# Second block of a two-block transformer on one core: a new order of its 48 attention steps and of the slabs beside them

## What is computed

```python
def hybrid_mixer(u, cos, sin, ...):
    (dq, dk, dv, nq, kc_, vc_, ks_, vs_, kw_, vw_, ngate, mgate) = jnp.split(u @ w_in, split_at, axis=-1)
    dq, dk = apply_rope(dq, c4, s4), apply_rope(dk, c4, s4)
    y_a = differential_attention(dq, dk, dv, lam)          # p[0] - lam * p[1], causal, 4 heads of 2
    y_a = rms_norm(y_a, diff_subln_g) * (1.0 - lam_init) @ w_branch_a
    nq = apply_rope(nq, c3, s3)
    k_cmp = compress(apply_rope(kc_), cmp_pe_k, cmp_k_w1, cmp_k_w2)   # silu(blk @ w1) @ w2, 31 blocks of 32 tokens
    v_cmp = compress(vc_, cmp_pe_v, cmp_v_w1, cmp_v_w2)
    o_c, o_s, o_w = nsa_attention(nq, k_cmp, v_cmp, k_sel, vs_, k_win, vw_)
    y_b = g[:, :, 0] * o_c + g[:, :, 1] * o_s + g[:, :, 2] * o_w
    return (mg[:, :, 0] * y_a + mg[:, :, 1] * (y_b @ w_branch_b)) @ w_out
```

## Time and profile before

| | us |
|---|---|
| median of 3 runs | 2106.61 (2105.53 to 2108.7) |
| the profiled execution | 2107.49 |
| its span in the trace | 2105.7 |
| TensorE busy with matmuls | 2037.0 (97% of the span) |
| VectorE / ScalarE / GpSimd busy | 967.5 / 902.7 / 870.4 |
| the 48 steps, step 0 to the end of step 48 | 1290.3 to about 1601 |

### The profile page before, as it was taken

One profiled execution on the slowest core, in us unless ns is written; L12 is line 12 of the kernel. 1 busy time (PEld: TensorE's weight loads), 2 busy tenths in 40 slices (PEclk: granted clock), 3 DMA queues, 4 the chain that ended last, 5 costly groups with the idle time before them and its releaser, 6 DMA issues.

```text
span 2105.7 us, 28470 instructions
## 1 busy us (share of the span) xinstructions
PE 2037.0 (97%) x9900; PEld 1604.6 (76%) x9900; DVE 967.5 (46%) x1559; ACT 902.7 (43%) x1760; POOL 870.4 (41%) x648
## 2 busy tenths in 40 slices
PE   9999999999999988899999999999999999999997
PEld 6777688888887755688888887766667888888886
DVE  6444545322255677542312255557655653323133
ACT  5444443333343654442323346656654333223234
POOL 3222354444454221254444454442113555445454
PEclk9999999999999999999999999999999999999999
DMA  4222123223222110122223322221111222323323
GB/s 156 71 71 81 59 92 101 93 97 100 93 96 90 61 41 31 41 91 100 100 91 99 100 90 80 94 97 41 41 41 62 99 92 99 100 91 100 100 90 110
DMA packets 50581, 177.88 MB, mean 84 GB/s; under 512 B 5536, under 2 KB 5800, under 8 KB 50480
## 3 DMA queue, kind: packets, MB, share of 16 engines
q1 hardware_dynamic: 48096, 172.07, 24.7%
q10 hardware_dynamic: 2384, 4.43, 0.7%
HBM read 174.36 MB, written 2.12 MB: 84 GB/s over the span
## 4 chain that ended last, share of the span: by engine, by line
issue 47%; PE 31%; POOL 19%; DVE 2%; POOLq 1%; ACT 0%; DVEq 0%; ACTq 0%
POOL w_lo L456 19%; PE gemm_banks L481 9%; PE gemm_banks L482 9%; PE gemm_banks L483 9%; PE score_banks L935 1%; PE out_bank L981 1%; PE score_banks L944 1%; DVE turned L2136 1%; POOLq L450 0%; POOLq L455 0%; PE gemm_banks L907 0%; DVE score_banks L1721 0%; DVE x L2232 0%; PE out_bank L972 0%; ACT tmp L1414 0%
## 5 line engine op out<-in xcount | busy, mean ns | idle before, releaser
L456 POOL TENSOR_TENSOR w_lo<-raw,w_hi 128x512 fp32r<-128x512 f32 x644 | 870.2, 1373 | 1218.1 <-ACT w_hi L1052 1218.0
L1052 ACT ACTIVATE w_hi<-raw 128x512 fp32r<-128x512 f32 x644 | 370.9, 623 | 824.5 <-PE gemm_banks L483 809.4
L481 PE MATMUL gemm_banks<-h_hi,w_hi 128*128 128x512 f32 x1512 | 611.3, 404 | 3.1 <-POOL w_lo L456 2.9
L483 PE MATMUL gemm_banks<-h_hi,w_lo 128*128 128x512 f32 x1512 | 590.5, 391 | 0.0
L482 PE MATMUL gemm_banks<-h_lo,w_hi 128*128 128x512 f32 x1512 | 589.7, 390 | 0.0
L481 PEld LDWEIGHTS gemm_banks<-h_hi,w_hi 128*128 128x128 f32 x1512 | 283.0, 187 | 93.8 <-issue 34.7
L481 PE MATMUL gemm_banks<-u_hi,w_hi 128*128 128x512 f32 x848 | 330.3, 390 | 4.2 <-POOL w_lo L456 2.9
L483 PEld LDWEIGHTS gemm_banks<-h_hi,w_lo 128*128 128x128 f32 x1512 | 282.8, 187 | 62.1
L483 PE MATMUL gemm_banks<-u_hi,w_lo 128*128 128x512 f32 x848 | 329.9, 389 | 0.0
L482 PE MATMUL gemm_banks<-u_lo,w_hi 128*128 128x512 f32 x848 | 329.9, 389 | 0.0
L482 PEld LDWEIGHTS gemm_banks<-h_lo,w_hi 128*128 128x128 f32 x1512 | 283.4, 187 | 56.3 <-issue 2.6
(11 more groups left out here) (316 smaller groups left out, 1889.8 us busy)
## 6 DMA issues: line engine op xcount, KB each, us to landing
raw<-slabs SPq DMA_DIRECT2D x322, 512.0 KB, 3.3
table<-rel_rows ACTq DMA_DIRECT2D x4, 512.0 KB, 3.8
x<-x_t SPq DMA_DIRECT2D x4, 256.0 KB, 6.7
x<-x_t ACTq DMA_DIRECT2D x4, 256.0 KB, 6.9
cos<-pos SPq DMA_DIRECT2D x2, 256.0 KB, 10.4
y_t<-x SPq DMA_DIRECT2D x2, 256.0 KB, 2.9
y_t<-x ACTq DMA_DIRECT2D x2, 256.0 KB, 2.7
y_t<-x SPq DMA_DIRECT2D x1, 512.0 KB, 2.8
```

The lines of the kernel that those rows point to most:

```text
L456: pool.tensor_tensor(w_lo[:, j, part], raw[:, j, part], w_hi[:, j, part].bitcast(F32), ALU.subtract).then_inc(slab_split, 1)
L481: pe.matmul(out, high, rhs_hi, start=first, stop=False)
L483: return pe.matmul(out, low, rhs_hi, start=False, stop=last)
L1052: act.activation(w_hi[:, m % 2, part], raw[:, m % 2, part], ACT.Copy).then_inc(slab_hi, 1)
```

## The change

1. `E_GROUPS`: the four slabs of `w1` are no longer used one after the other. One slab of `w1` now stands between two full slabs: w1(0) with q2, k2, v2, and w1(1) with q3, k3, v3, ks. The slabs are packed in that order. `E_TURNS` puts `tk` 0, `w2` 0, `vt` 3, and all `cs` and `pct` later by one to four halves.
2. VectorE: where half 2s ends fewer than two results, `e_take(s-1)` comes straight behind `maxima(s)`, and `e_half(2s)` behind it. The sum of a rotation comes one place later: of half 2s behind the take of the next step, of half 2s - 1 at the end of step s.
3. ScalarE: `e_swaps(2s-1)` comes behind `e_half(2s)` and the scaling of the shares instead of ahead of them.
4. The rounding of the second compressed block (`blocks_high`, `e_blocks_low`) comes two halves later.

```diff
--- before.py
+++ after.py
@@ -216,24 +216,29 @@
 
 
 E_BASE, DIFF_STEPS, E_STEPS, E_AHEAD = 64, 16, 48, 6
+
 E_GROUPS = [(6, (("q", 0), ("k", 0), ("v", 0), ("kc", 0))), (6, (("vc", 0), ("q", 1), ("k", 1), ("v", 1))),
-            (4, (("w1", 0),)), (4, (("q", 2), ("k", 2), ("v", 2))),
-            (6, (("q", 3), ("k", 3), ("v", 3), ("ks", 0))), (4, (("w1", 1),)),
+            (8, (("w1", 0, 0), ("q", 2), ("w1", 0, 1), ("k", 2), ("w1", 0, 2), ("v", 2), ("w1", 0, 3))),
+            (10, (("q", 3), ("w1", 1, 0), ("k", 3), ("w1", 1, 1), ("v", 3), ("w1", 1, 2), ("ks", 0), ("w1", 1, 3))),
             (8, (("ng", 0), ("nq", 0), ("kw", 0), ("vs", 0), ("vw", 0))),
             (64, (("nq", 1), ("b", 0), ("b", 1), ("nq", 2), ("b", 2), ("b", 3), ("nq", 3),
                   ("b", 4), ("b", 5), ("b", 6), ("b", 7)))]
-E_TURNS = [("vt", 0, -1), ("vt", 1, 7), ("tk", 0, 11), ("ns", 0, 12), ("w2", 0, 14), ("vt", 2, 15), ("ns", 1, 20),
-           ("vt", 3, 20), ("tk", 1, 25), ("gt", 0, 27), ("w2", 1, 28), ("ns", 2, 28), ("cs", 0, 30), ("vst", 0, 31),
-           ("pct", 0, 33), ("vwt", 0, 34), ("ns", 3, 36), ("cs", 1, 41), ("pct", 1, 44), ("cs", 2, 58),
-           ("pct", 2, 61), ("cs", 3, 75), ("pct", 3, 78)]
+E_TURNS = [("vt", 0, -1), ("vt", 1, 7), ("ns", 0, 12), ("tk", 0, 15), ("vt", 2, 15), ("w2", 0, 18), ("ns", 1, 20),
+           ("vt", 3, 21), ("tk", 1, 25), ("gt", 0, 27), ("w2", 1, 28), ("ns", 2, 28), ("cs", 0, 31), ("vst", 0, 31),
+           ("pct", 0, 34), ("vwt", 0, 34), ("ns", 3, 36), ("cs", 1, 43), ("pct", 1, 46), ("cs", 2, 60),
+           ("pct", 2, 63), ("cs", 3, 77), ("pct", 3, 80)]
 ROTATED = ("q", "k", "kc", "ks", "kw", "nq")
 
 
 def plan_e():
     halves = []
     for n, items in E_GROUPS:
-        tiles = [(name, p, j, 2 * KT if name == "w1" else KT) for name, p in items
-                 for j in range(2 * KT if name == "w1" else KT)]
+        tiles = []
+        for name, p, *quarter in items:
+            if name == "w1":
+                tiles += [(name, p, 4 * quarter[0] + j, 2 * KT) for j in range(4)]
+            else:
+                tiles += [(name, p, j, KT) for j in range(KT)]
         halves += [tiles[len(tiles) * k // n:len(tiles) * (k + 1) // n] for k in range(n)]
     inside = {}
     for name, p, target in E_TURNS:
@@ -1432,7 +1437,7 @@
                             gemm_slab()
                         taken_out[name, p] = c.gemm.at()
                         e_end(name, p)
-                if h == 11:
+                if h == 13:
                     blocks_high(1)
 
             def e_square(p):
@@ -1461,13 +1466,13 @@
                     e_mixed((s - DIFF_STEPS - 9) // 8)
                 if s < E_STEPS:
                     weigh(E_BASE + s, e_step(s)[3])
-                if s > 0:
-                    e_swaps(2 * s - 1)
                 e_half(2 * s)
                 if s < DIFF_STEPS:
                     e_halve(s)
                 elif s < E_STEPS:
                     even(s, e_step(s)[3], 48 + s + 1)
+                if s > 0:
+                    e_swaps(2 * s - 1)
                 e_swaps(2 * s)
                 e_half(2 * s + 1)
             e_mixed(3)
@@ -2121,7 +2126,7 @@
                 if h == 4:
                     e_blocks(1)
                     link(dve.memset(pcT[64:128, :, :], 0.0))
-                if h == 12:
+                if h == 14:
                     e_blocks_low(1)
 
             def e_take(s):
@@ -2173,16 +2178,25 @@
                     maxima(E_BASE + s, e_step(s)[3], [sin1[:, S - e_step(s)[3]:S]] * 2)
                 if s % 8 == 1 and s > DIFF_STEPS + 8:
                     e_mixed((s - DIFF_STEPS - 9) // 8)
-                e_half(2 * s)
+
+
+                ahead = len(ends_of(2 * s)) < 2
+                if not ahead:
+                    e_half(2 * s)
                 if s >= 1:
                     e_take(s - 1)
-                e_rotated(2 * s - 1)
+                    e_rotated(2 * s - 2)
+                else:
+                    e_rotated(-1)
+                if ahead:
+                    e_half(2 * s)
                 if s < E_STEPS:
                     e_shares(s)
                 e_half(2 * s + 1)
                 if s < DIFF_STEPS:
                     e_combine(s)
-                e_rotated(2 * s)
+                if s >= 1:
+                    e_rotated(2 * s - 1)
             e_mixed(3)
             c.hi.now += KT
             c.lo.now += KT
@@ -2299,10 +2313,11 @@
     of["nq"] = lambda p: [w[:, 1536 + pair_cols[p]]]
     of["b"] = lambda p: [w[:, 3864 + P * p:3864 + P * (p + 1)]]
     for n, items in E_GROUPS:
-        for name, p in items:
+        for name, p, *quarter in items:
             if name == "w1":
                 t = tiles_of(a[("cmp_k_w1_2", "cmp_v_w1_2")[p]][0])
-                out += [np.ascontiguousarray(t[:, 4 * q:4 * q + 4]).reshape(P, SLAB) for q in range(4)]
+                q = quarter[0]
+                out.append(np.ascontiguousarray(t[:, 4 * q:4 * q + 4]).reshape(P, SLAB))
             else:
                 out += [slab(t) for t in of[name](p)]
     w_b = a["w_branch_b_2"][0][np.concatenate(pair_cols)]
```

## The result

| | before | after |
|---|---|---|
| median | 2106.55 us (6 runs, 2105.53 to 2108.7) | 2121.4 us (6 runs, 2117.47 to 2122.68) |
| profiled execution, its span | 2107.49, 2105.7 | 2121.62, 2119.8 |
| idle time of TensorE in the steps | 22.4 | 31.0 |
| time at the lower clock in the steps | 17.1 in 4 stretches | 30.7 in 7 stretches |

The ratio is 1.0068, with a 95% interval of 1.0056 to 1.0080. The direction was forecast; the size was not (forecast +5.8, measured +14.8, which is next to the rival "more low clock" with its 2122). The median lies 0.4 us above the upper end of the stated range, 2121, and outside the forecast's own range of 2107 to 2118.

What follows compares the result with a forecast made beforehand. TensorE was taken as the bound, busy 2037.0 of 2105.7 us, with only idle and low-clock time to win. Terms -18.0, +12.2, +9.6 and clock +2 gave +5.8 us, a forecast of 2112.4 us, range 2093 to 2121.

Steps and rivals of the forecast that it cites:

- more low clock: Rival: a low-clock stretch after each of seven gaps over 1 us, three operations stretched; 2122 us, chance 0.11.
- What is removed: TensorE's waits that should go: w1 slabs 7.7, copies 3.6, `cs` 4.4, scaled shares and the 0.7 together 2.3; -18.0 us.
- Gaps of steps 3 to 12, +12.2: New TensorE waits ahead of full slabs behind w1 slabs, whose cover is short; q2 the largest at 3.85; +12.2 us.
- Steps 13 to 48, +9.6: New waits from later exchanges, sums and take-outs: nq1, nq2, step 18, vst 0, pct 0, nq3; +9.6 us.
- The waits at nq1 and nq2: Steps 20 and 29: exchange behind scaling and sum ahead of maxima delay turned shares; +3.8 and +3.1 us.
- nq3's gain: Steps 36 to 38: its sum goes behind the next take; step 38 starts some 3 us earlier against step 36.
- 3 x 1.1: Three new gaps may hold a VectorE operation stretched by GpSimd's work; +3.3 us, left out of the sum.
- the 2081 of the first rival: Time if the cover is enough and the waits at nq1 and nq2 stay away too; 2081 us.
- the clock, +2: One single low-clock stretch more than before, from one less to three more; +2 us, between -2 and +5.
- the 2.37 without a stretch: Old TensorE wait of 2.37 us, ahead of `cs`, which no low-clock stretch followed; used to price the clock.
- The cover is enough: Rival: splits in steps 3 to 12 come about 2.5 us earlier, most of the 12.2 goes; 2093 us, chance 0.25.
- Half comes back: Rival: engines catch up in the early gaps, or nq1's and nq2's sums cost half; 2104 to 2109 us, chance 0.17.

Runs made afterwards that it cites:

- x5_cs: The kernel before with the later places of `cs` and `pct` alone; 2110.13 us, ratio 1.0012.
- x1_interleave: The kernel before with w1's slabs between full slabs and the places of `tk`, `w2`, `vt` 3 and the blocks, nothing else; 2101.36 us, ratio 0.9974.
- a2_no_ahead: The changed kernel with VectorE's take of the turned shares behind the results of half 2s again; 2107.97 us, ratio 1.0009.
- a1_block: The changed kernel with the second compressed block and its memset made in half 5 instead of half 4; 2115.36 us, ratio 1.0037.
- c1_late_sum: The changed kernel with the sum of an odd half's rotation behind the next step's take from step 17 on; 2114.14 us, ratio 1.0031.
- y5_block_pct: Interleaved w1 with the old orders to step 16, then the change's orders with later odd-half sums; block in half 5, pct 3 two halves later; 2099.53 us.

## Why the prediction was right in direction and short in size

- **What is removed.** Right for w1's own matmuls (7.7) and `cs` (4.4): neither group has a wait left. Wrong in two points: the 0.7 for L944's `probs` stays (0.7, L949), and of the waits for copies 4.0 stay instead of 3.2. x5_cs adds that the 4.4 was never to be had from the places alone.
- **Gaps of steps 3 to 12, +12.2.** Measured 13.9 (12.4 for `w_lo`, 1.2 for KT, 0.3 for VT), less 0.9 for a wait in step 1 that went: +13.0. q2's first product started at 1323.24, as worked out (1323.2); TensorE came 1 us earlier since that wait was gone, and the chain, which began earlier too, was held up by the sum of 1.68 us that I had at 0.6. q3 3.17 (2.8), v3 2.91 (2.4), ng 1.09 (1.1), v2 1.15 (1.3, though for its bank and not for `w_lo`).
- **Steps 13 to 48, +9.6.** Here lies most of what the idle term lacks: with what goes, forecast -0.7, measured +3.4. The waits at nq1 and nq2 came as forecast (3.53 and 2.58 against 3.8 and 3.1), and nq3's gain as well (step 38 starts 4.4 us earlier against step 36 than before; 1.1 of that is `cs` 3 itself, which stands behind the start of step 38 now). vst 0 is 2.03 instead of 0.95, because VectorE's remainder `u_lo` ahead of VT took 1.76 us beside GpSimd's work (0.68 at its shortest). The 1.93 ahead of pct 3 was not foreseen at all; instead of it I had 0.55 at pct 0, which did not come. Both have an operation in them that GpSimd's work stretched. The bound that I left out of the sum for this, 3 x 1.1, belonged into it: the three places, q2, vst 0 and pct 3, measured 1.1 + 1.1 + 2.0 = 4.2 us. That the three would meet GpSimd's work "for certain" did not follow from the rule named there, which tells only what happens where they meet. Small waits for scaled shares add 1.1, the wait for `probs` that stayed 0.7, those for copies 0.8. (Two slips in the working change nothing in the sum: "the other six full slabs" are seven, and the 2081 of the first rival stands without its sum.)
- **The step that failed most plainly: the clock, +2.** Measured +6.8 in the same count. The idle term was 4.8 short (3.8 against 8.6), the clock term 4.8 as well. I had counted one single stretch more than the four before, one of which was double; there were seven, two of them double, so three single lengths more than I had. The rival came nearer (each of the large gaps has a stretch), and I gave it 0.11. That it met the time to 1 us is in part luck: two of its seven gaps, v2 and ng, had no stretch, and vst 0 and pct 3, which it did not have, did. The row that I leaned on, the 2.37 without a stretch, is one draw. Over the fourteen profiles of this study a stretch began in the gap or within 2 us behind it for 23 of 26 gaps of 2.5 us and more, for 14 of 36 of those between 1.5 and 2.5, and for 4 of 74 of those between 0.8 and 1.5. By these counts the gaps that I had forecast (q2, q3, nq1, nq2 over 2.5 us, v3 between, four small ones) give 4.1 stretches, and those measured (five, two and three) 5.4. So one stretch or so came from gaps larger than forecast. That there were seven, and two of them double, these counts don't explain; it seems to recur from run to run, since five of the six executions lie between 2121.1 and 2122.7 at a mean granted clock of 0.989 to 0.990.
- **The two other rivals.** "The cover is enough" asked whether the interleaving pays at all; x1_interleave shows that it does (-5.5) where VectorE and ScalarE keep their order. "Half comes back" did not show.

What stays open: why the 2.90 us gap of a2_no_ahead and two of about 3 us in other kernels (2.91 in a1_block, 3.16 in c1_late_sum) were not followed by a stretch, and why some stretches are double (and one in a2_no_ahead, at its 2.58 us gap, triple: 10.2 us). And part of the 11 to 12 us that only the two halves together cost is clock that falls differently; I have not separated it run by run.

## What to carry to other kernels

An engine that is told to take a late result first stands idle before it, with finished work behind it in its own list. Ahead of moving a step up, ask what the engine would have done in the wait, and whose chain that work feeds; here the rule of one line cost 13 us, and a sum that waited for an exchange ahead of the maxima 7. Close the account with two terms, idle time and half of the low-clock time: a gap over 2.5 us costs its length and here mostly 1.7 to 3.4 us more, so splitting one large gap into small ones pays although the sum of waits hardly moves.

## What the runs showed of the hardware

VectorE and GpSimd hold each other up by whole instructions. A VectorE operation on 8 columns with both operands in SBUF took 0.17 us alone and 1.23 beside GpSimd's remainder, one on 256 columns 0.42 and 1.38, one on 512 columns 0.69 and 1.68, the block of 992 columns 1.88 and 2.87 (y5_block_pct). What is added is neither a share of the length nor a fixed time; it is what was left of GpSimd's instruction. In the changed kernel the same operation on 2 columns (`share<-share,gates`, 0.16 alone) took 0.22, 0.30, 0.52 and 0.90 us, and each time it ended 0.02 us behind GpSimd's instruction. In the fourteen traces 2271 such operations on 512 columns (sums and products of two tensors) started with 0.15 to 1.29 us left of an instruction of GpSimd; all of them ended 0.54 to 0.56 us behind its end. The other way round, the second part of a remainder that started under the block's 1.97 us in a2_no_ahead took 2.83 us instead of 1.28. With one operand in a bank nothing is held up: `VT<-gemm_banks,rstd`, 512 columns, took 0.68 with 1.20 us of GpSimd's instruction left.

The spread of one kernel's times goes with the clock: of eight runs of c1_late_sum two took 2109.8 and 2110.08 us, at a mean granted clock of 0.994, and six 2113.96 to 2114.57, at 0.991. In the profiled one of 2109.8 the low-clock time outside the steps is 12.4 us, where the other profiles have 13.8 to 22.3.
